# Expert loop of a two-layer decoder step: TensorE takes the halves of its two products in turn

## What is computed

```
act = jax.nn.gelu(jnp.einsum('td,tjd->tj', xb, u_tab[eidx]).astype(jnp.float32), approximate=False)
return jnp.einsum('tj,tjd->td', (gate * act).astype(xb.dtype), v_tab[eidx])
```

## Time and profile before

| what | value |
| --- | --- |
| median of 3 runs | 5084.44 us (5082.71 to 5089.52) |
| the profiled execution | 5096.14 us |
| its span, first to last instruction | 5094.3 us |
| expert loop from its first `output` on, layer 0 | 1507 to 2549 us of the span |
| the same, layer 1 | 4034 to 5076 us of the span |
| PE busy | 3915.0 us, 77% of the span |
| DVE busy | 3642.8 us, 72% |
| POOL busy | 2533.1 us, 50% |
| read from main memory | 805.56 MB |

### The profile page before, as it was taken

One profiled execution on the slowest core, in us unless ns is written; L12 is line 12 of the kernel. 1 busy time (PEld: TensorE's weight loads), 2 busy tenths in 40 slices (PEclk: granted clock), 3 DMA queues, 4 the chain that ended last, 5 costly groups with the idle time before them and its releaser, 6 DMA issues. The chain is left out here.

```text
span 5094.3 us, 77114 instructions
## 1 busy us (share of the span) xinstructions
PE 3915.0 (77%) x29074; PEld 3577.1 (70%) x29074; DVE 3642.8 (72%) x5442; ACT 1549.5 (30%) x2740; POOL 2533.1 (50%) x1244
## 2 busy tenths in 40 slices
PE   6966484852569999999979654848425699999998
PEld 5945484851459999999969444847424699999997
DVE  2064634488979999999920646345889799999998
ACT  2131211211234444444321322112112344444443
POOL 2300010224678888888722001012267788888886
PEclk9966676986789999999989667769767899999999
DMA  3111001101479999999821200012014899999997
GB/s 110 61 54 34 2 12 42 61 17 33 97 220 341 339 341 342 337 342 344 301 75 56 68 15 2 12 42 69 9 43 99 260 345 337 340 344 340 338 343 271
DMA packets 474206, 870.83 MB, mean 171 GB/s; under 512 B 223072, under 2 KB 279200, under 8 KB 473088
## 3 DMA queue, kind: packets, MB, share of 16 engines
q1 hardware_dynamic: 363392, 465.13, 27.4%
q0 software_dynamic: 110592, 402.70, 21.6%
HBM read 805.56 MB, written 61.58 MB: 170 GB/s over the span
## 5 line engine op out<-in xcount | busy, mean ns | idle before, releaser
L2104 DVE SCALAR_TENSOR_TENSOR arena<-arena 128x1024 f32<-128x1024 f32 x384 | 1024.8, 2669 | 1.7 <-DMA arena<-u_rows,arena 1.7
L2030 POOL TENSOR_TENSOR u_split<-arena,u_split 128x1024 fp32r<-128x1024 f32 x256 | 685.3, 2677 | 116.7 <-ACT u_split L1977 114.0
L154 PE MATMUL ps<-x_split,u_split 128*128 128x384 f32 x2048 | 689.3, 337 | 54.0 <-POOL u_split L2030 53.9
L156 PE MATMUL ps<-x_split,u_split 128*128 128x384 f32 x2048 | 688.6, 336 | 0.0
L155 PE MATMUL ps<-x_split,u_split 128*128 128x384 f32 x2048 | 687.8, 336 | 0.0
L2023 POOL DMA_INDIRECT arena<-u_rows,arena x384 | 620.9, 1617 | 121.5 <-issue 65.3
L2074 PE MATMUL ps<-w_split,c_split 128*128 128x512 f32 x1536 | 600.1, 391 | 0.0
L2073 PE MATMUL ps<-w_split,c_split 128*128 128x512 f32 x1536 | 599.8, 390 | 0.0
L2072 PE MATMUL ps<-w_split,c_split 128*128 128x512 f32 x1536 | 597.4, 389 | 0.0
L2026 POOL DMA_INDIRECT arena<-pk_v,arena x384 | 463.5, 1207 | 165.0 <-DVE arena L2112 84.8
L335 POOL TENSOR_TENSOR w_split<-arena,w_split 128x2048 fp32r<-128x2048 f32 (+1 forms) x54 | 245.7, 4555 | 529.5 <-ACT w_split L329 529.5
(11 more groups left out here) (367 smaller groups left out, 8491.6 us busy)
## 6 DMA issues: line engine op xcount, KB each, us to landing
arena<-pk_u SPq DMA_DIRECT2D x256, 512.0 KB
arena<-pk_v SPq DMA_DIRECT2D x256, 512.0 KB
g_scratch<-arena SPq DMA_DIRECT2D x24, 2048.0 KB, 11.3
arena<-g_scratch SPq DMA_DIRECT2D x128, 384.0 KB
arena<-w_in SPq DMA_DIRECT2D x28, 1024.0 KB, 5.4
arena<-pk_wq SPq DMA_DIRECT2D x16, 1024.0 KB, 6.3
arena<-cache_k SPq DMA_DIRECT2D x32, 256.0 KB, 2.7
arena<-cache_v SPq DMA_DIRECT2D x32, 256.0 KB, 3.3
```

The lines of the kernel that those rows point to most:

```text
L154: pe.matmul(out, lhi, rhi, start=(n == 0), stop=False)
L156: last = pe.matmul(out, llo, rhi, start=False, stop=(n == len(terms) - 1))
L2030: pool.tensor_tensor(us[:, e, 1], u_raw[:, e], us[:, e, 0].bitcast(F32), ALU.subtract).then_inc(u_ready, 1)
L2104: dve.scalar_tensor_tensor(ug[:, m], ug[:, m], 1.0, xt[:, member[m]], ALU.mult, ALU.mult, accum_out=hid[:, m:m + 1]).then_inc(dot_done, 1)
```

## The change

The functions `hidden` and `output` on PE lose their loop over the halves and take e as an argument; the loop over e now stands outside of them. In a pair's turn PE did both halves of `hidden` of the next pair and then both halves of `output` of this one. Now it does half 0 of `hidden`, half 0 of `output`, half 1 of `hidden`, half 1 of `output`. The first pair's `hidden` and the last pair's `output` still have both halves one after the other. What each half waits for and signals is the same, and the instructions of the other engines are the same and in the same order.

```diff
-                    def hidden(k, first=False):
-
-                        for e in range(2):
-                            pe.wait_ge(u_ready, k * 2 + (e + 1))
...
+                    def hidden(k, e, first=False):
+
+                        pe.wait_ge(u_ready, k * 2 + (e + 1))
...
-                    def output(k, s, first=False, last=False):
-
-                        for e in range(2):
-                            pe.wait_ge(v_ready, k * 2 + (e + 1))
-                            pe.wait_ge(c_ready, k * 2 + (e + 1))
...
+                    def output(k, s, e, first=False, last=False):
+
+                        pe.wait_ge(v_ready, k * 2 + (e + 1))
+                        pe.wait_ge(c_ready, k * 2 + (e + 1))
...
                     pe.sem_inc(o_done, 2)
-                    hidden(0, True)
-                    hidden(1)
-                    output(0, 0, first=True)
+                    for e in range(2):
+                        hidden(0, e, True)
+                    for e in range(2):
+                        hidden(1, e)
+                        output(0, 0, e, first=True)
                     with pe.Fori(0, PAIRS // 2 - 1) as i:
                         for s in range(2):
-                            hidden(i * 2 + (s + 2))
-                            output(i * 2 + (s + 1), 1 - s)
-                    output(PAIRS - 1, 1, last=True)
+                            for e in range(2):
+                                hidden(i * 2 + (s + 2), e)
+                                output(i * 2 + (s + 1), 1 - s, e)
+                    for e in range(2):
+                        output(PAIRS - 1, 1, e, last=True)
```

More of the change, by code:

```diff
@@ L2076, in _ @@
-                    pe.sem_inc(o_done, 2)
-                    hidden(0, True)
-                    hidden(1)
-                    output(0, 0, first=True)
+                    def hidden(k, e, first=False):
+                        pe.wait_ge(u_ready, k * 2 + (e + 1))
+                        if not first:
+                            pe.wait_ge(c_ready, k * 2 + (e - 1))
+                        split_products(pe, ps[:, e, 0:DENSE],
+                                       [((us[:, e, 0, c * P:(c + 1) * P], us[:, e, 1, c * P:(c + 1) * P]),
+                                         (x_part(0)[:, c, 0:DENSE], x_part(1)[:, c, 0:DENSE])) for c in range(KC)]).then_inc(h_done, 1)
@@ new lines, in output @@
+                    def output(k, s, e, first=False, last=False):
+                        pe.wait_ge(v_ready, k * 2 + (e + 1))
+                        pe.wait_ge(c_ready, k * 2 + (e + 1))
+                        for i in range(DT):
+                            for n in range(2):
+                                o = ps[:, 2 + 2 * i + n, :]
+                                ch_, cl = (cs[:, s, e, h, i * P:(i + 1) * P] for h in range(2))
+                                vh, vl = (vs[:, s, e, h, n * 512:(n + 1) * 512] for h in range(2))
+                                pe.matmul(o, ch_, vh, start=first and e == 0, stop=False)
+                                pe.matmul(o, ch_, vl, start=False, stop=False)
+                                done = pe.matmul(o, cl, vh, start=False, stop=last and e == 1)
+                        done.then_inc(o_done, 1)
```

## The result

The changed kernel takes 5100.39 us (median of nine runs; a tenth, at a granted clock of 0.76 where the others had 0.86, took 5345.81 us and is left out) against a median of 5083.57 us of ten runs of the kernel before, measured beside it. The ratio is put at 1.0029 [1.0016, 1.0042], that is 14.7 us more, with an interval from 8 to 21; the two medians by themselves lie 16.8 us apart. The change makes the kernel slower by about 0.3%, with an interval clear of 1, and the time is within the predicted range of 5086 to 5104.

The account below looks back on a forecast made before the run. PE (TensorE), which never waits in the expert loop once started, was taken as the bound. Switches +8.4, loop's end +4.5 and loop's start -0.4 gave +12.5 us on 5084.44, so 5096.9 us; range 5086 to 5104.

Parts of the forecast that it names:

- Switches, +8.4: PE in the expert loops: 252 more changes between first and second product at 0.033 us each, +8.4 us.
- The mean of the two kinds: Price per change of product on PE, averaged over first-to-second and second-to-first: 0.067 / 2 = 0.033 us.
- The rival that switches are free: The 0.067 us on PE comes once per pair, so only the loop's ends count: 5088.5 us, chance 0.18.
- The loop's end, +4.5: Last first-product half comes 4.12 us later, so DVE's closing chain ends past PE: +2.25 and +2.24 us per layer.
- The loop's start, -0.4: O(0,0), ready long before, now stands ahead of H(1,1), which waits for c: 0.11 + 0.27 us saved.
- What was costed at nothing: Inside the loop, the later second GELU shifts DVE, POOL and loads, but remaining cover keeps PE from stalling: 0 us.
- The rival in which POOL becomes the bound: In the loop, shifted phases make POOL collide with DVE more often: 81 us more, some 5177 us, chance 0.08.

Follow-up runs that it names:

- equal columns: First product widened from 384 to 512 columns, extra columns wasted, in the order of the kernel before and in the changed order: 5399.94 and 5406.75 us.
- the loop alone: Halves alternate as in the changed kernel, except that the last pair keeps the order of the kernel before; against the kernel before 1.0016, 5098.14 us.
- without the last mixes: The changed kernel with DVE's last three mixes left out, the last gathers still issued: 5103.53 us, one execution.
- the last pair alone: The kernel before, with only the last `hidden` alternating by halves with the `output` ahead of the last one; against the kernel before 1.0012, 5095.08 us.
- the later gathers: The kernel before, with the first pair's gathers of v moved behind the second pair's u work on POOL; against the kernel before 1.0000, 5087.91 us.

## Why the prediction was right, and where it was off

The forecast was 12.5 us more, the medians say 14.7 [8, 21], and the two profiled loops 12.9. Term by term:

**Switches, +8.4: confirmed.** The mean of the two kinds was the right value between the bounds of 0 and 16.9: pairs 16.613 apart as forecast (16.61), with halves of 4.19 and 4.12 in the rows above, 8.1 us in the run that had this part alone, and the same 0.033 at runs half as long. The trace shows the two kinds apart: over the even pace, a run of H takes 0.026 us more and a run of O 0.041, whether it is 12, 24 or 48 matmuls of H or 9, 18 or 36 of O. Their mean was the right price because the new order adds as many of each and the loss does not depend on the length of the run. The rival that switches are free falls with the spacing of the pairs. What the prediction did not know is why. It spoke of a change of product; the runs with equal columns show that the loss goes with the change of column count. By the rule of the Trainium skill that was weighed ("TensorE: Matmul & The Clock Gate", section Back-to-back issue gap) the term would be 0, since it prices a matmul by its own columns and, in a stream, by its weight load, with nothing for the matmul ahead of it. The trace contradicts it where 384 and 512 columns meet, and agrees, as far as the change of product goes, where all have 512.

**The loop's end, +4.5: the mis-sized term. It measured +6.5** (5.68 - 2.43 = 3.25 and 5.65 - 2.42 = 3.23). What the prediction said of DVE came true: PE is done 2.10 us ahead of DVE's last mix, 2.25 forecast. The step that failed is that DVE's mix would close the stage. POOL's drain closes it. The trace of before had it already, in a view that was not read for the sum, the closing instructions at L126 of the kernel before:

```profile
L126 POOLq DRAIN  x2: 34/4530/9027, 2539.6 to 2551.6; - x2
```

It ended at 2539.6 + 9.03 = 2548.63, later than DVE's 2547.41 and only 0.65 ahead of PE's 2549.28, and so hid behind PE. Moved by the same 4.12 us it would have been forecast at 3.47 past PE; it came 3.3 past (2546.24 - 2542.92). The chain is the one that the prediction described, H(63,1), the mixes that free the buffers, the last gathers; only its last link was another. The packet records of the gathers' queue show how both links hang on the gathers: the last packet landed at 2545.80 before and at 2543.40 after the change, 3.48 us ahead of PE's end and 0.48 us behind it. DVE's last mix is done 1.6 us after that packet, POOL's drain 2.8.

**The loop's start, -0.4: it measured -1.8, by a fall of the clock that did not come in layer 1.** From H(1,0) to the half behind it took 5.98 us in layer 0 (1496.65 to 1502.63) and 5.97 in layer 1. After the change these rows of PE's timeline stand behind H(1,0):

```profile
1492.13 0.40 PE L2070 MATMUL ps<-w_split,c_split 128*128 128x512 f32 x1
...
4015.45 0.39 PE L2070 MATMUL ps<-w_split,c_split 128*128 128x512 f32 x1
```

That is 1492.13 - 1486.28 = 5.85 in layer 0, a gain of 0.13 where 0.11 was forecast; in layer 1 it is 4.27, a gain of 1.70 where 0.27 was forecast. The windows over H(1,0) say why, layer 1 of before and then of after (same columns as above):

```profile
4023.80:4029.30 5.50, 5.50 (x23) 5.50 (x24) 5.50 (x6) 1.65 (x3) 5.24 (x3) 0.72 0.98 378
```

```profile
4011.20:4015.40 4.20, 4.20 (x24) 4.20 (x25) 4.20 (x4) 0.95 (x2) 4.10 (x2) 1.00 1.03 407
```

In layer 1 of after TensorE ran H(1,0) at the full 2.4 GHz (1.00) from its first matmul, after a wait of 2.20 us; before, the clock was at 1.2 GHz for most of it (0.72 over the window), after a wait of 3.66 us; layer 0 of after also had a low clock (0.71), after 2.84 us. The new order is needed for the gain too: before, in layer 0, H(1,1) started at 1502.63, 0.15 us after DVE had made the c that it waits for, and that c comes from pair 0 and not from H(1,0). A faster H(1,0) would there have ended in a longer wait; this is argued from the rows and was not run. As for the fall, the other profiles add to it. Of the six loops that start as the changed kernel's do (this one, the loop alone, and without the last mixes), the clock fell in two, after waits of 2.84 and 4.19 us, and stayed up in four, after waits of 2.01 to 2.50, with 4.27 to 4.29 us from H(1,0) to O(0,0). In the eight loops that start as before (both profiles of that kernel, the last pair alone, and the later gathers), it fell in all, after waits of 3.12 to 4.19. Nothing that the change moves stands ahead of H(1,0), so whether it has a part in the shorter waits stays open.

By the terms as measured the two loops give 8.4 + 6.5 - 1.8 = 13.1, and the cut from the profiles was 12.9. That this is so near the forecast's 12.5 is in part luck: the end was forecast 2.0 too low and the start 1.4 too high, and the two nearly cancel.

**What was costed at nothing: it cost nothing.** A pair of the changed kernel: H(20,0) starts at 1803.60 (1504.57 + 18 x 16.613), the next one at 1820.22. Timelines of DVE and of POOL:

```profile
1809.92 0.55 DVE L2094 TENSOR_TENSOR ps<-ps,arena 128x384 f32<-128x384 f32 x1
...
1812.88 3.05 DVE L2106 SCALAR_TENSOR_TENSOR arena<-arena 128x1024 f32<-128x1024 f32 x1 [0.81 <-DMA arena<-u_rows,arena]
...
1816.88 0.57 DVE L2094 TENSOR_TENSOR ps<-ps,arena 128x384 f32<-128x384 f32 x1 [0.94 <-ACT ps L1993]
```

```profile
1812.42 2.42 POOL L2030 TENSOR_TENSOR u_split<-arena,u_split 128x1024 fp32r<-128x1024 f32 x1
```

As forecast, DVE no longer waits at the first product and waits for the GELU at the second, 0.94 us. POOL's first `u_lo` is done at 1814.84, 5.4 us ahead of the H that needs it; 4.4 was forecast as what is left of 7.6. The rival in which POOL becomes the bound did not come: PE waits for nothing in the loop. Not foreseen was that DVE also waits for gathered rows of u (0.81 us here). The dots by line, first of before and then of after (busy us and mean ns of one, then idle time before it and what ended most of it):

```profile
L2104 DVE SCALAR_TENSOR_TENSOR arena<-arena 128x1024 f32<-128x1024 f32 x384 | 1024.8, 2669 | 1.7 <-DMA arena<-u_rows,arena 1.7
```

```profile
L2106 DVE SCALAR_TENSOR_TENSOR arena<-arena 128x1024 f32<-128x1024 f32 x384 | 718.8, 1872 | 82.5 <-DMA arena<-u_rows,arena 82.0
```

The dots became shorter by 306 us in all; the mixes became longer by 214 (483.8 to 697.8 us busy), and 80 us of new waiting for rows of u stands ahead of the dots. Why is not followed here. It bought nothing and cost nothing, because the loop does not wait for DVE.

## What to carry to other kernels

On a TensorE that never waits, count the places where the number of columns changes from one matmul to the next: each cost 0.033 us here, between 384 and 512, and 126 more of them 0.4% of a loop. At the end of a stage look for whatever is done last on *every* engine, the sequencers' closing instructions included; work that ends 0.65 us ahead of the bound becomes the bound when its chain is moved by 4. And a profile's span is no measure of a change when the rest of the program scatters by 20 us: cut the changed stage out.

## What the runs showed of the hardware

- A change between matmuls of 384 and 512 columns costs TensorE 0.067 us per two changes, at run lengths of 9 to 48 matmuls: 0.026 in the run of 384 and 0.041 in the run of 512. With 512 columns throughout, a change of product, operands and banks costs nothing (226.7 ns per matmul).
- POOL's drain at the loop's end follows the landing of the gathers. In all twenty loops of the ten profiles it ends 2.78 to 2.84 us after the last packet of the gathers' queue, while its distance from the end of the last issue varies from 6.8 to 7.5 us. In the changed kernel DVE's last mix starts at 2543.74, 0.34 us after that packet, and so is done ahead of the drain. The drain ends at the same distance where no mix uses the last rows. What fills the 2.8 us is left open. The table has the times to the hundredth from the trace's records; the views above round a drain's start to a tenth.

| kernel, layer 0 | last gather issued until | its queue's last packet | POOL's drain ends | after that packet |
| --- | --- | --- | --- | --- |
| before | 2541.62 | 2545.80 | 2548.59 | 2.8 |
| changed | 2539.33 | 2543.40 | 2546.21 | 2.8 |
| the loop alone | 2533.11 | 2537.72 | 2540.56 | 2.8 |
| last pair alone | 2544.68 | 2548.78 | 2551.62 | 2.8 |
| without the last mixes | 2541.18 | 2545.17 | 2547.97 | 2.8 |
